# A modulation split between two stages, a causal mask moved from TensorE to GpSimd, joint decays, and four buffers for a streamed weight

## The reference, cut to what matters

```python
sh1, sc1, g1, sh2, sc2, g2 = split(silu(cvec) @ w_ada + b_ada, 6)      # w_ada: 1024 x 6144
h  = rmsnorm(x, n1) * (1 + sc1) + sh1
mq, mk, mv, mo, gt, aq, ak, av = split_cols(h @ w_in)                  # w_in: 1024 x 2832
# mLSTM, chunkwise, forward and backward; per head:
d = where(lower, b[l] - b[s] + ig[s], -inf); m_t = max(b + m, max(d))
s = (q @ k.T) * exp(d - m_t);  num = s @ v + exp(b + m - m_t) * (q @ C)
C_new = decay * C + sum(g * k * v)                                     # decay = exp(b[-1] + m - m_new)
x = x + g1 * (concat(mlstm_out, attention_out) @ w_out)
h2 = rmsnorm(x, n2) * (1 + sc2) + sh2
x = x + g2 * peer(h2)          # q = h2 @ w_q, top-k of product keys, 128 experts per token gathered
```

## Time and profile before

| | us |
|---|---|
| median of three runs (lowest to highest) | 3905.86 (3894.59 to 3912.28) |
| profiled execution | 3902.2 |
| its span, first to last instruction | 3900.4 |
| PE busy / DVE busy / POOL busy / ACT busy | 2771.2 / 2357.3 / 1451.6 / 968.6 |
| mean granted TensorE clock | 0.842 of full speed |
| indirect DMA of the expert phase | 1208.03 MB of 1371.88 MB |

### The profile page before, as it was taken

The page is one execution under the profiler, slowest core; times in us unless marked ns, Lnnn a source line. Parts: engine busy times, 40 slices in busy tenths (PEclk is TensorE's granted clock), DMA queues, the critical chain, the costliest instruction groups (busy, mean ns, idle before and its releaser), DMA issues.

```text
span 3900.4 us, 31656 instructions
## 1 busy us (share of the span) xinstructions
PE 2771.2 (71%) x10020; PEld 1088.1 (28%) x10020; DVE 2357.3 (60%) x5323; ACT 968.6 (25%) x2686; POOL 1451.6 (37%) x1287
## 2 busy tenths in 40 slices
PE   6899988867878788856576567567557656755555
PEld 1455465733333343312122112112112111211111
DVE  1334332664785686637767757856866775785554
ACT  1122222233343443312122122122112212211111
POOL 0000011243444444434444444444444444444443
PEclk6899979878999998879798788779779878977777
DMA  9211154398999999999999999999999999999998
GB/s 412 81 61 50 46 174 151 114 374 355 402 360 419 420 404 370 400 365 421 399 421 421 410 421 421 407 422 421 417 408 421 420 405 421 421 399 421 422 422 369
DMA packets 221781, 1371.88 MB, mean 352 GB/s; under 512 B 24882, under 2 KB 35762, under 8 KB 70066
## 3 DMA queue, kind: packets, MB, share of 16 engines
q0 software_dynamic: 165888, 1208.03, 75.3%
q1 hardware_dynamic: 47956, 138.32, 9.4%
q10 hardware_dynamic: 7776, 23.60, 1.5%
HBM read 1338.79 MB, written 31.07 MB: 351 GB/s over the span
## 4 chain that ended last, share of the span: by engine, by line
DMA 40%; PE 21%; DVE 13%; POOL 4%; issue 4%; ACT 4%; SPq 1%; ACTq 0%; DVEq 0%; POOLq 0%
DMA fx_ring<-arg_uv,fx_eidx 37%; PE fx_acc L1301 11%; DVE fx_ring L1725 7%; POOL fx_ring L1026 4%; PE at_sP L1153 3%; ACT fx_weighted_pick L1441 2%; DMA rt_wq<-arg_w_q 2%; PE at_aP L1115 1%; DVE rt_rest L1601 1%; PE rt_qP L1176 1%; DVE rt_ab L1603 1%; DVE rt_rest L1599 1%; ACT fx_gelu L1437 1%; PE at_sP L1099 1%; SPq L973 1%
## 5 line engine op out<-in xcount | busy, mean ns | idle before, releaser
L1301 PE MATMUL fx_acc<-fx_ring,fx_weighted_pick 128*64 128x512 f32 x4608 | 1444.9, 760 | 988.9 <-ACT fx_weighted_pick L1441 967.5
L1026 POOL DMA_INDIRECT fx_ring<-arg_uv,fx_eidx x1152 | 1330.4, 1155 | 1719.4 <-PE fx_acc L1301 1520.2
L1725 DVE CUSTOM_DVE_ANT_0 fx_ring<-fx_ring,fx_h 128x1024 f32<-128x1024 f32 x1152 | 1403.4, 1230 | 809.3 <-DMA fx_ring<-arg_uv,fx_eidx 804.8
L1301 PEld LDWEIGHTS fx_acc<-fx_ring,fx_weighted_pick 128*64 128x64 f32 x4608 | 330.0, 160 | 1974.6 <-ACT fx_weighted_pick L1441 1426.5
L1437 ACT ACTIVATE fx_gelu<-fx_dot 128x2 f32<-128x2 f32 x576 | 117.1, 203 | 2124.1 <-DVE fx_dot L1725 2119.3
L1441 ACT ACTIVATE fx_weighted_pick<-fx_weighted_pick,fx_gelu 128x64 f32<-128x64 f32 x1152 | 338.2, 340 | 54.3 <-ACT fx_gelu L1437 1.1
L432 PE MATMUL in_z<-w_in,in_hT 128*128 128x512 f32 (+1 forms) x864 | 348.2, 561 | 1.7 <-ACT in_hT L465 1.7
L432 PEld LDWEIGHTS in_z<-w_in,in_hT 128*128 128x128 f32 x864 | 162.8, 191 | 168.6 <-issue 160.9
L1176 PE MATMUL rt_qP<-rt_w_q,rt_h2T 128*128 128x512 f32 x384 | 195.3, 633 | 0.0
L1153 PE MATMUL at_sP<-at_w_out,at_mixT 128*128 128x512 f32 x288 | 134.9, 612 | 2.1 <-ACT at_mixT L1333 1.3
L390 POOL COPY in_turned<-in_heads 128x320 f32<-128x320 f32 x9 | 4.1, 452 | 271.7 <-DVE in_heads L557 271.7
(11 more groups left out here) (282 smaller groups left out, 2465.6 us busy)
## 6 DMA issues: line engine op xcount, KB each, us to landing
ada_w<-arg_w_ada SPq DMA_DIRECT2D x24, 1024.0 KB, 9.8
rt_wq<-arg_w_q SPq DMA_DIRECT2D x48, 512.0 KB, 7.8
fx_ring<-arg_uv,fx_eidx POOLq DMA_INDIRECT x1152
w_in<-arg_w_in SPq DMA_DIRECT2D x8, 1416.0 KB, 22.0
ml_qkT<-qkT_scratch SPq DMA_DIRECT2D x18, 512.0 KB, 3.6
rt_w_q<-arg_w_q SPq DMA_DIRECT2D x16, 512.0 KB, 20.2
kv_scratch<-in_kv ACTq DMA_DIRECT2D x9, 768.0 KB, 3.3
ada_x<-arg_x ACTq DMA_DIRECT2D x9, 512.0 KB, 8.1
```

The source lines that it names most:

```text
L1026: pool.indirect_dma_start(out=ring[j][:], out_offset=None, in_=io.uv, in_offset=bass.IndirectOffsetOnAxis(ap=eidx[t % 2][:, i:i + 1], axis=0),
L1301: mm = pe.matmul(acc[b][cg * TOKS:(cg + 1) * TOKS, :], wsel[:, i % (2 * FILL), :], ring[i % GROUP][:, D + b * 512:D + (b + 1) * 512], star ...
L1725: dve.tensor_tensor_reduce(out=ring[j][:, 0:D], in0=ring[j][:, 0:D], in1=h2r[t % 2][cg][:], scale=1.0, scalar=0.0, op0=ALU.mult, op1=ALU.a ...
```

## The change

**Conditioning.** Only parts 0 and 1 (shift and scale of the first norm) are made before the projection: eight chunks of w_ada, each with a buffer of its own, then x tile 0, then w_in. The ACT squares, `rstd`, PE's spread of gates and their stores are gone from this stage. **Projection.** Parts 2 to 5 are summed on DVE: for each of 32 chunks of 128 x 1024 and each of two conditions one `scalar_tensor_tensor` adds weight times SiLU value into an accumulator, four chunks a tile in tiles 0 to 7. In tiles 2, 4, 6 and 8 PE sums the accumulator over partitions by a column of ones (`ada_out`) and DVE takes the result. The norm of x is made tile by tile (ACT square, DVE, ACT root, DVE), and the turn of the next x stands behind block K instead of Q. The gate rows are stored once (4 KB) and spread by the loading DMA. **mLSTM.** The mask matmul is replaced by a select on POOL between ACT's exponential and DVE's product. From unit 3 on the decays come from one matmul and one exponential for all tiles. **route(0).** w_q runs through four buffers (two new ones lie in space of `h2r[0]`).

```diff
@@ conditioning @@
-                for c in range(GROUPS * KD):
-                    grp, k = divmod(c, KD)
-                    if c >= RING:
-                        sp.wait_ge(s_mm, c - RING + 1)
-                    sp.dma_start(wbuf[c % RING][:], io.w_ada[k * P:(k + 1) * P, grp * GC:(grp + 1) * GC]
-                                 ).then_inc(s_w[c % RING], 16)
+                for k in range(KD):
+                    sp.dma_start(wbuf[k][:], io.w_ada[k * P:(k + 1) * P, 0:GC]).then_inc(s_w[k // 2], 16)
+                sp.dma_start(g.xn[:], io.x[0]).then_inc(g.s_x, 16)
                 for k in range(KD):
                     sp.dma_start(g.w_in[:, k, :], io.w_in[k * P:(k + 1) * P, :]).then_inc(g.s_w_in, 16)
-                for i in range(2 * COND):
-                    sp.wait_ge(s_rowe, 2 * i + 2)
-                    sp.dma_start(g.gate_dram[i], gate[i]).then_inc(s_gst, 16)
-                sp.wait_ge(s_gst, 32 * COND)
...
@@ project_in, SP @@
+                def ada(t):
+                    if t % 2 == 0 and t:
+                        n = t // 2 - 1
+                        if PARTS[n] in (2, 5):
+                            sp.wait_ge(s_ae, n + 1)
...
+                        for m in range(t * EACH, (t + 1) * EACH):
+                            if m >= AW:
+                                sp.wait_ge(s_a, COND * (m - AW + 1))
+                            k = m % KD
+                            sp.dma_start(ada_w[m % AW][:], io.w_ada[k * P:(k + 1) * P, o:o + D]).then_inc(s_aw[m % AW], 16)
@@ project_in, PE @@
-                        if b == 2 and not last:
+                        if b == 1 and t and t % 2 == 0:
+                            pe.wait_ge(s_attTd, t)
+                            ada_out(t // 2 - 1)
+                        if b == 3 and t >= 2:
+                            pe.wait_ge(s_ae, t // 2)
+                        if b == 3 and not last:
                             turn_x(t + 1)
...
+                def ada_out(n):
+                    pe.wait_ge(s_a, COND * (n + 1) * KD)
+                    for cnd in range(COND):
+                        if PARTS[n] in (3, 4):
+                            for k in range(KD):
+                                mm = pe.matmul(akTp[:, 3 * P + k * COND + cnd:3 * P + k * COND + cnd + 1],
+                                               ada_acc[cnd][:, k * P:(k + 1) * P], one[:], start=True, stop=True)
+                        else:
+                            for half in range(2):
+                                mm = pe.matmul(xTp[half][32 * cnd:32 * cnd + 1, :], one[:],
+                                               ada_acc[cnd][:, half * 512:(half + 1) * 512], start=True, stop=True)
+                    mm.then_inc(s_at, 1)
@@ project_in, DVE @@
+                    for cnd in range(COND):
+                        dve.scalar_tensor_tensor(ada_acc[cnd][:], ada_w[m % AW][:], g.silu[:, k, cnd:cnd + 1],
+                                                 ada_b[:] if k == 0 else ada_acc[cnd][:], ALU.mult, ALU.add).then_inc(s_a, 1)
@@ mix_and_experts, POOL and PE of a unit @@
+                            pool.wait_ge(s_e, u + 1)
+                            turn = 1 if d == 0 else -1
+                            pool.affine_select(out=ew[d][:], in_=ew[d][:], compare_op=ALU.is_ge, fill=0.0, base=0,
+                                               pattern=[[0, MH], [turn, P]], channel_multiplier=-turn).then_inc(s_em, 1)
...
-                            pe.matmul(eP[:, h, :], g.sel[side, h, :], g.cum[side, ti * P:ti * P + P], start=(h == 0), stop=False)
-                        mask = g.neg_after if d == 0 else g.neg_before
-                        pe.matmul(acc[0][:], g.ident[:], mask[:].rearrange("p h n -> p (h n)"),
-                                  start=False, stop=True).then_inc(s_eP, 1)
+                            mm = pe.matmul(eP[:, h, :], g.sel[side, h, :], g.cum[side, ti * P:ti * P + P], start=True, stop=True)
+                        mm.then_inc(s_eP, 1)
...
@@ mix_and_experts, SP, w_q @@
-                        if m >= WQ:
-                            sp.wait_ge(s_qd, m - WQ + 1)
+                        if m >= ahead(m):
+                            sp.wait_ge(s_qd, max(m - ahead(m), NSIDE - 1 if m >= NSIDE else 0) + 1)
...
-                for m in range(WQ):
+                for m in range(2 * WQ):
                     chunk(m)
```

More of the change, by code:

```diff
@@ L160, in _ @@
             @block.tensor
             def _(pe):
-                pe.wait_ge(s_silu, 1)
+                pe.wait_ge(s_dve, 3)
                 pe.wait_ge(s_small, 48)
-                for grp in range(GROUPS):
-                    for k in range(KD):
[L166 to L184, removed]
[L185 to L196 removed]
+                pe.wait_ge(s_const, 1)
@@ L370, in _ @@
                 sp.dma_start(io.new_kv, g.new_kv[:]).then_inc(g.s_m0, 16)
-                with sp.Fori(1, TILES - 1) as t:
-                    tile(t)
-                tile(TILES - 1, True)
+                for t in range(1, TILES):
+                    tile(t, t == TILES - 1)
+                    ada(t)
                 sp.wait_ge(g.s_m0, 48)
+                sp.wait_ge(s_gst, 16 * 2 * COND)
             @block.gpsimd
@@ L579, in tile @@
                                       bg[:].rearrange("p (d s r) -> p s d r", d=2, s=2), ALU.add).then_inc(s_att, 1)
+                    for m in adds[1:2]:
+                        ada_add(m)
+                    if not last:
+                        scaled(t + 1, 1 - par, 1)
+                    for m in adds[2:]:
+                        ada_add(m)
                     if not first:
@@ new lines, in _ @@
+                ca = Count(dve, s_ac)
+                dve.memset(one[:], 1.0)
+                ca.link(dve.memset(ada_b[:], 0.0))
+                dve.wait_ge(s_xsq, 1)
+                dve.tensor_scalar(rms[:, QKH:QKH + 1], rms[:, QKH:QKH + 1], 1.0 / ADH, EPS, ALU.mult, ALU.add).then_inc(s_rt_in, 1)
+                dve.wait_ge(s_rt, 1)
+                dve.reciprocal(rms[:, QKH:QKH + 1], rms[:, QKH:QKH + 1]).then_inc(s_xr, 1)
+                scaled(0, 0, 0)
+                for t in range(TILES):
+                    tile(t, t % 2, first=t == 0, seed=t == 1, last=t == TILES - 1)
@@ L834, in mix_and_experts @@
         s_att = sem("at_dve_chain")
[L836 removed]
+        s_wq = [sem(f"rt_wq_in{i}") for i in range(2 * WQ)]
         s_wqr = [sem(f"rt_w_q_in{i}") for i in range(2)]
@@ L1687, in back_rows @@
                                               g.mprev[back, 1:TILES].unsqueeze(2).to_broadcast([32, TILES - 1, P]), ALU.add))
-                    dve.tensor_copy(g.rows[1][32:32 + MH, lat], g.inter[new, lat]).then_inc(g.s_rows, 1)
+                    dve.tensor_copy(g.rows[1][32:32 + MH, lat], g.inter[new, lat])
+                    for r in range(2):
+                        part = slice(32 * r, 32 * r + MH)
+                        end = P - 1 if r == 0 else 0
+                        last = dve.tensor_tensor(ends[part, r], chunks(g.inter[part, :])[:, :, end].unsqueeze(1).to_broadcast([MH, MH, TILES]),
+                                                 g.ident[part, part].unsqueeze(2).to_broadcast([MH, MH, TILES]), ALU.mult)
+                    last.then_inc(g.s_rows, 1)
                 def begin():
```

328 lines of the change are left out of this document (181 added, 147 removed).

## The result

The changed kernel takes 3786.5 us (median of 4 runs, 3775.7 to 3792.0), the kernel before 3901.1 beside it; the ratio is 0.970, 95% interval 0.967 to 0.973. The profiled execution of the changed kernel was its fastest, 3775.7, some 11 under its median; its span is 3774.0.

A forecast was written before the change was run, and what follows sets the result against it. Loads bound the first stage, PE the projection, nothing alone the mixing stage; the expert part's 3,100 us only start earlier. -51 + 16 - 26 = -61 from 3905.9 gives 3845 us, range 3819 to 3875.

The forecast's parts named there:

- The first stage, -51: Before the projection: fewer loads ahead of w_in move the first projection matmul from 119.2 to 68.1 us, -51.
- Rival (e): First stage: projection's start hangs on something other than the loads, such as code fetch; -10 instead of -51, 3886; chance 0.05.
- The projection, +16: Projection: PE gains two row parts at 3.5 us and two column parts at 4.6, all on the path; +16.
- (b): Projection: DVE late, sums' loads and POOL's locks push hT or gate rows past most tiles' end; +32, 3877; chance 0.12.
- (d): Projection: DVE becomes the bound if a sum takes over 2.2 us; at 3.4 us it costs 77, 3922; chance 0.04.
- The mixing stage, -26: mLSTM, mixer and route(0), projection's end to experts: -12 - 10 - 10 + 1 + 5 = -26, bounds -38 and -5.
- mask: Mixing stage: PE drops the mask matmul, 1.13 us per unit in seven dense units; last units save 10; forecast -16.
- decays: Mixing stage: PE drops decays from unit 3 on, 1.05 us per unit, hidden in the last units; forecast -6.
- buffers: route(0): four w_q buffers remove PE's waits of 9.9 us; 1 is lost to 1 MB more queued ahead of other loads.
- The clock allowance: Mixing stage: +5 (0 to +25) in case PE's granted clock stays at 0.50 without the mask matmul.
- Rival (a): Mixing stage: with mask and decays gone, 545 to 770 us runs mostly at clock 0.50; +25, 3870; chance 0.13.
- Rival (c): Small loads do not queue and PE's relief comes through whole: -62 + 14 - 34 = -82, 3824; chance 0.10.

The follow-up runs named there:

- e2: Changed kernel with an unused tensor of 64 bytes a partition right ahead of the ring (the expert phase's eight gather buffers); 3819.9 us, ratio 0.980.
- e9: Changed kernel with DVE's wait for the small loads (in_g, in_bg) moved from ahead of its memsets to ahead of the first tile; 3779.0 us, ratio 0.969.
- e12: Changed kernel with the edit of e9 and PE's wait for w_in moved behind the turn of the first x; 3769.0 us, ratio 0.967.
- e5: Changed kernel with w_q's chunks in two buffers again; from the projection's last turn to the first expert fetch +17.5 us against the changed kernel.
- e4: Changed kernel with 512 unused bytes a partition ahead of the expert phase's gather buffers; 3793.7 us, one execution.
- e10: Changed kernel with 128 unused bytes a partition ahead of the expert phase's gather buffers; 3819.9 us, one execution.
- e11: Changed kernel with 256 unused bytes a partition ahead of the expert phase's gather buffers; 3792.1 us, one execution.
- e3: Changed kernel with an unused 2 MB scratch tensor in HBM ahead of kv_scratch, later scratch tensors standing as in the kernel before; 3775.9 us, one execution.
- e6: Changed kernel with the mask on TensorE again and no select on GpSimd; from the projection's last turn to the first expert fetch +19.1 us.

## Why the prediction was wrong, point by point

**The step that failed** is a sentence of the first paragraph: "The change doesn't touch that last part: its 3,100 us only start earlier." It touches where the ring stands. Of the 58 us between forecast and median (3845 and 3786.5), 30 to 38 are this. Without it, in e2, the changed kernel takes 3819.9, just inside the range (from 3819). By parts, the profiled execution lies 65 below its forecast of 3841: 48.4 in the expert part (36 by the place, about 12 scatter), 15.5 in the mixing stage and 1.4 in the projection. The median gives 7 of the 65 back (below). I had no rival with another expert part, so no chance covered it; the one mark that caught it was "if the expert part changes its length by over 10".

The row was there to be weighed: 421 GB/s in the earlier trace rows against 425 in the earlier trace rows, where another queue wrote other tiles. And a page had the rule. The Trainium skill (DMA: Bandwidth & Descriptors, "How a descriptor splits into AXI transactions") says that a descriptor (the order for one run of bytes) which does not start on a 256-byte boundary begins with a transaction from the boundary below, whose unused bytes still cost. It words this for what is read; here the side that moved is the one written. The boundary agrees with the runs: 0 at 427, 64, 128 and 192 at 421. The size does not. An estimate by its count of 32-byte beats gives 258, 260 and 262 for a row of 8,192 bytes against 256, so 0.8, 1.6 and 2.3%; the runs have 1.4% for each. The measurement decides, and why the loss is the same for all three offsets stays open.

**The first stage, -51: right,** at -51.1, by the mechanism named (DVE's first memset at 54.50, 54.6 forecast). e9 and e12 show the chain: take DVE's wait away and w_in is the next. Rival (e) is out.

**The projection, +16: right in sum,** +14.6, with two terms off that cancel in part. The two row parts took 1.89 us each instead of 3.5: I priced them by passes with 128 output rows, while the earlier trace rows had the nearer row, eight passes of 512 columns with two output rows in 1.88; the column parts took 3.63 and 4.43 instead of 4.6. The rest, 2.6 us, is the clock behind the second column part (below). DVE's sums took 1.28 to 1.47 us and none held PE, whose only wait was the first `hT`; rivals (b) and (d) are out. The lock between DVE and GpSimd, which the prediction put on one of the sums, showed on a rotation product instead: L560 took 2.07 us beside GpSimd's scaling of x, its neighbours of the same shape 0.82.

**The mixing stage, -26: right in its parts, too small by 15.** By the experiments: mask -19 (forecast -16), decays -11 (-6), buffers -17.5 (-9 with the queue's +1), less 4 of overlap, and no loss by the clock, for which I had allowed +5. The term furthest off is the buffers: I priced PE's waits at their length. The clock allowance and the decays follow, 5 us each. Rival (a), the clock, is out. Rival (c) had the full relief but not the start.

**The median.** The changed kernel's median stands 10.8 us above its profiled execution, which was the fastest of four; the forecast had carried over the 3.7 of the kernel before. That this took 7 us off the miss is luck.

## What to carry to other kernels

When a change adds or drops a tensor, work out where the buffers above it now start, and do so first for the buffers that the bounding transfers write: here 64 bytes in an unrelated stage were worth about a quarter of the gain, and a pad of one line gives it to the old kernel too. A part that a change "doesn't touch" deserves a chance of its own when it is 80% of the time. And waits of PE in a dense stretch can cost more than their length: 17 us for 11 in e5.

## What the runs showed of the hardware that I had not expected

**The gathers into SBUF ran 1.4% slower off a 256-byte boundary,** rows of 8,192 bytes, 421 against 427 GB/s, whatever the offset of the three tried. e2, e4, e10 and e11 move the ring and all that stands above it together; that the ring carries the loss is argued from its being what the full queue writes.

**The clock can fall while PE is busy without a gap.** Behind the 32 one-column matmuls at 328.62 the changed kernel's windows are:

```profile
333.00:335.00 2.00, 2.00 (x4) 0.97 (x4) 1.97 (x4) 0.00 (x0) 1.44 (x2) 0.50 0.00 0
335.00:337.00 2.00, 2.00 (x3) 0.76 (x3) 2.00 (x3) 0.00 (x0) 2.00 (x2) 0.50 0.00 0
337.00:339.00 2.00, 2.00 (x5) 0.73 (x4) 1.97 (x2) 0.00 (x0) 1.23 (x1) 0.73 0.68 186
```

PE was 100% busy throughout, with full matmuls from 332.90 on, and ran at 0.50 (1.2 GHz) to some point past 337. Behind the same group at 244.22 the clock held. Where it falls differs from run to run. In e3 both groups took 3.63 us and the 32 full passes behind each took 15.68:

```profile
247.55 15.68 PE L392 MATMUL in_z<-w_in,in_hT 128*128 128x512 f32 x32
```

Against 3.63 and 13.98 us, the two groups and the 32 passes behind each cost 3.4 us more in all in eight of the twelve profiles that have them (the changed kernel, e3 and six others), and 5.0 in e4, e6, e10 and e12; the latter four have the longer projections (381.3 to 381.7 us, the others 378.9 to 379.5). Behind the two row parts the same 32 passes took 14.00 in all twelve. So the loss comes with the one-column matmuls, but no run took them apart. The rule that the prediction weighed, that sustained activity releases the throttle (the Trainium skill, TensorE: Matmul & The Clock Gate, "Part 1: The HAM clock gate"), does not tell these rows apart: PE was as busy at 244 as at 328. What decides stays open.
